# The second block's recurrence by pairs of tiles, its gates read from PSUM by ScalarE, its norm applied ahead, and output slabs begun three in step

## What is computed

```python
xn = rmsnorm(x, norm_mix_g)                    # the third norm of the whole kernel
u, g_lru, q, k, v, z = split(xn @ w_in)        # u, g_lru: 1024 wide each; z: 2048 (za, zb)
uc = conv4(u)                                  # centred depthwise convolution
r = sigmoid(uc @ wa + ba); i = sigmoid(uc @ wx + bx)       # 64-wide blocks, for each of two directions
a = exp(-8 * r * softplus(-lam)); beta = sqrt(1 - a * a)
h = scan(h_prev * a + beta * (i * uc))         # forwards and backwards over the tokens
y_a = (h_fwd + h_bwd) * gelu(g_lru)
y_b = banded_attention_with_sink(q, k, v)
merged = sigmoid(za + b) * y_a + sigmoid(zb + b) * y_b
x = x + merged @ w_out
x = x + (silu(gate) * up) @ w_ffn_out          # of rmsnorm(x) @ w_ffn_in
return rmsnorm(x, norm_final)
```

## Time and profile before

| | |
|---|---|
| median of 3 runs | 1547.47 us (1546.45 to 1548.66) |
| the profiled execution's own time | 1548.28 us |
| its span, first to last instruction | 1546.5 us |
| mean granted TensorE clock | 0.974 of full |
| busy: TensorE matmuls | 1448.2 us, 94% |
| busy: VectorE / ScalarE | 881.1 us, 57% / 638.3 us, 41% |
| DMA | 131.6 MB, mean 85 GB/s |

### The profile page before, as it was taken

One profiled execution on the slowest core, in us unless ns is written; L12 is line 12 of the kernel. 1 busy time (PEld: TensorE's weight loads), 2 busy tenths in 40 slices (PEclk: granted clock), 3 DMA queues, 4 the chain that ended last, 5 costly groups with the idle time before them and its releaser, 6 DMA issues.

```text
span 1546.5 us, 17781 instructions
## 1 busy us (share of the span) xinstructions
PE 1448.2 (94%) x7272; PEld 1166.9 (75%) x7272; DVE 881.1 (57%) x1267; ACT 638.3 (41%) x994; POOL 1.9 (0%) x7
## 2 busy tenths in 40 slices
PE   6997899998999999999899999978899999999997
PEld 6876577777778888888687777756678888888886
DVE  5775564566544445364647877578874443443445
ACT  4445465333222222123425667778743321222232
POOL 0000000000000000000000000000000000000000
PEclk9998899999999999999899999989999999999998
DMA  4211222222133323233131111122233332333323
GB/s 157 87 65 42 92 91 64 85 93 82 60 109 96 98 94 108 84 96 106 43 109 55 52 45 56 55 68 68 68 109 96 96 98 93 96 97 108 92 86 109
DMA packets 36561, 131.64 MB, mean 85 GB/s; under 512 B 4432, under 2 KB 4560, under 8 KB 36224
## 3 DMA queue, kind: packets, MB, share of 16 engines
q1 hardware_dynamic: 36128, 127.16, 26.4%
q0 software_dynamic: 352, 3.34, 0.6%
HBM read 128.39 MB, written 2.10 MB: 84 GB/s over the span
## 4 chain that ended last, share of the span: by engine, by line
PE 69%; DVE 16%; ACT 11%; issue 3%; DMA 1%; SPq 0%; DVEq 0%; ACTq 0%
PE gp L1351 20%; PE gp L1353 20%; PE gp L1352 20%; DVE w_lo L783 2%; PE mp L1527 1%; ACT arena L706 1%; PE mp L1538 1%; ACT w_hi L414 1%; DVE arena L1006 1%; PE mp L1499 1%; DVE arena L1013 1%; ACT a_hi L441 1%; ACT arena L563 1%; PE mp L1380 1%; ACT arena L710 1%
## 5 line engine op out<-in xcount | busy, mean ns | idle before, releaser
L1351 PE MATMUL gp<-a_hi,w_hi 128*128 128x512 f32 x1120 | 443.8, 396 | 14.2 <-DVE arena L1244 13.0
L1352 PE MATMUL gp<-a_lo,w_hi 128*128 128x512 f32 x1120 | 439.0, 392 | 0.0
L1353 PE MATMUL gp<-a_hi,w_lo 128*128 128x512 f32 x1120 | 438.3, 391 | 0.0
L783 DVE TENSOR_TENSOR w_lo<-raw,w_hi 128x1024 fp32r<-128x1024 f32 x232 | 283.5, 1223 | 168.1 <-ACT w_hi L414 166.9
L414 ACT ACTIVATE w_hi<-raw 128x1024 fp32r<-128x1024 f32 x232 | 243.3, 1052 | 197.3 <-PE gp L1353 105.1
L1351 PEld LDWEIGHTS gp<-a_hi,w_hi 128*128 128x128 f32 x1120 | 212.2, 189 | 66.5 <-DVE w_lo L783 16.5
L1353 PEld LDWEIGHTS gp<-a_hi,w_lo 128*128 128x128 f32 x1120 | 212.1, 189 | 45.1
L1352 PEld LDWEIGHTS gp<-a_lo,w_hi 128*128 128x128 f32 x1120 | 212.2, 189 | 42.6
L1351 PE MATMUL gp<-h_hi,w_hi 128*128 128x512 f32 x576 | 224.9, 390 | 8.9 <-DVE h_lo L817 3.5
L1353 PE MATMUL gp<-h_hi,w_lo 128*128 128x512 f32 x576 | 224.1, 389 | 0.0
L1352 PE MATMUL gp<-h_lo,w_hi 128*128 128x512 f32 x576 | 224.1, 389 | 0.0
(11 more groups left out here) (236 smaller groups left out, 1438.5 us busy)
## 6 DMA issues: line engine op xcount, KB each, us to landing
raw<-slabs SPq DMA_DIRECT2D x232, 512.0 KB, 3.5
arena<-x_in SPq DMA_DIRECT2D x4, 512.0 KB, 6.2
arena<-x_in POOLq DMA_DIRECT2D x1, 2048.0 KB, 8.2
out_t<-arena SPq DMA_DIRECT2D x8, 256.0 KB, 2.1
arena<-bias POOLq DMA_DIRECT2D x1, 1024.0 KB, 5.9
arena<-s5b SPq DMA_DIRECT2D x1, 512.0 KB, 9.1
arena<-s5c SPq DMA_DIRECT2D x1, 512.0 KB, 10.0
par<-params SPq DMA_DIRECT2D x1, 232.0 KB, 2.6
```

The source lines that it names most:

```text
L783: TT(w_lo[:, n % RING, :], raw[:, n % RAW, :], w_hi[:, n % RING, :].bitcast(F32), ALU.subtract).then_inc(w_lo_ready, 1)
L1351: pe.matmul(dst, hi, x_hi(t), start=t == 0, stop=False)
L1352: pe.matmul(dst, hi, x_lo(t), start=False, stop=False)
L1353: ins = pe.matmul(dst, lo, x_hi(t), start=False, stop=t == tiles - 1)
```

## The change

1. **Recurrence by pairs in two sets of buffers.** `lru[0]` and `lru[1]` each hold decay, input and beta for both directions. ScalarE takes the eight sigmoids of a pair, then its four tanh, four exponentials, two square roots; VectorE works on both directions in one 1024-wide instruction and scans into UC. HS is gone. The clamp at zero moves into the constant `decay_tanh`.
2. **Gates as they come.** ScalarE takes each gate product from PSUM as tanh of half of it (sigmoid(x) = (1 + tanh(x/2))/2), VectorE applies it with one instruction as (1 + tanh) * y, and the factor a half is in the split of the merged value. Likewise ScalarE takes u (copy) and g (gelu) from PSUM.
3. **The third norm applied ahead of 36 slabs** (16 of u and g, 20 of mix): VectorE multiplies x by gain and R and both engines split it into h, one chunk per slab beside the last eight q, k, v slabs. `uc` and the merged value are split into a, the fourth norm's input into h.
4. **Order of slabs.** `STAGE` replaces `MIX`: zb of tile 0 is multiplied inside attention's last unit, then each recurrence slab is followed by the four gate slabs of its own pair (three for the first).
5. **Outputs begin three in step** (`start_stage("out2", ..., 3, 5)`), with the third in an `mp` bank; splits run three ahead there.

The diff, cut to its core (the old bodies of the mix loops are in the listing above; the remaining hunks change counters and which of the buffers a and h is named):

```diff
@@ -61,6 +62,14 @@
 for _t in range(DC):
     MIX += ([("lru", _t // 2)] if _t % 2 == 0 else []) + [("zb", _t)] + ([("za", _t - 1)] if _t else [])
 MIX += [("za", DC - 1)]
+WINDOWS = [[("za", 0), ("zb", 1), ("za", 1)]]
+WINDOWS += [[(kind, t) for t in (2 * j, 2 * j + 1) for kind in ("zb", "za")] for j in range(1, DC // 2)]
+STAGE = [("zb", 0)]
+for _j, _gates in enumerate(WINDOWS):
+    STAGE += [("lru", _j)] + _gates
+assert sorted(STAGE) == sorted(MIX)
@@ -71,6 +80,8 @@
 ORDER = list(range(NSLAB))
 for _k in range(8):
     ORDER[SLAB["u2"] + 2 * _k], ORDER[SLAB["u2"] + 2 * _k + 1] = SLAB["u2"] + _k, SLAB["g2"] + _k
+for _i, _key in enumerate(STAGE):
+    ORDER[SLAB["mix"] + _i] = SLAB["mix"] + MIX.index(_key)
-MIX_SLAB = {key: SLAB["mix"] + i for i, key in enumerate(MIX)}
-MIX_OUT = {key: OUT["mix"] + i for i, key in enumerate(k for k in MIX if k[0] != "lru")}
-MIX_GATE = [g for t in range(1, DC + 1) for g in [("zb", t - 1)] + ([("za", t - 2)] if t > 1 else [])] + [("za", DC - 1)]
+MIX_SLAB = {key: SLAB["mix"] + i for i, key in enumerate(STAGE)}
+MIX_GATES = [key for key in STAGE if key[0] != "lru"]
+MIX_OUT = {key: OUT["mix"] + i for i, key in enumerate(MIX_GATES)}
...
-        HS = region(15360, DC, T)
         logit2 = [region(15360, 4, 3 * P), region(16896, 4, 3 * P)]
         PT2 = region(18432, 3, T)
         nd8 = region(19968, 3 * P)
-        lru = [region(12288 + T * i, T) for i in range(6)]
-        lru45 = region(12288 + 4 * T, 2 * T)
+        lru = [{key: region(12288 + 6 * T * i + 2 * T * x, 2, T) for x, key in enumerate(("decay", "input", "beta"))}
+               for i in range(2)]
...
+        START_OUT2 = 3
...
-                if _name in ("ff", "q2") and 2 <= _k < START_BANKS:
+                if _name in ("ff", "q2", "out2") and 2 <= _k < START_BANKS:
                     PLACE[_o] = mp, _k - 2
                 elif _name in ("gate_s", "u2", "g2"):
                     PLACE[_o] = gp, 0
+                elif _name == "mix":
+                    PLACE[_o] = gp, (_k + 1) % 2
                 else:
                     PLACE[_o] = gp, _o % 2
...
-            for n in range(SLAB["q2"] + START, SLAB["u2"]):
-                split(n + AHEAD)
+            for c in range(DC):
+                split(SLAB["q2"] + START + c + AHEAD)
+                act.wait_ge(h_norm, NORMALISED_AT + c + 1)
+                nc.scalar.activation(h_hi[:, c, :], tmp[c % 2], ACT.Copy).then_inc(h_hi_ready, 1)
...
             def inputs2(u):
                 m = u // 2
-                if u % 2:
-                    act.wait_ge(h_val, V_AT["uc"] + m + 1)
-                    nc.scalar.activation(h_hi[:, m, :], UC[:, m, :], ACT.Copy).then_inc(h_hi_ready, 1)
-                    act.wait_ge(out_read, OUT["u2"] + u + 1)
-                    nc.scalar.activation(G2[:, m, :], G2[:, m, :], ACT.Gelu_apprx_tanh).then_inc(gate_val, 1)
+                if u % 2 == 0:
+                    take("u2", u, tmp[m % 2])
+                    return
+                act.wait_ge(h_val, V_AT["uc"] + m + 1)
+                nc.scalar.activation(a_hi[:, m, :], UC[:, m, :], ACT.Copy).then_inc(a_hi_ready, 1)
+                take("u2", u, G2[:, m, :], func=ACT.Gelu_apprx_tanh)
             attention(att2, SLAB["u2"], inputs2)
...
+            ahead = itertools.count(SLAB["mix"] + AHEAD)
             def mix_gate(kind, t):
-                row, bias = {"za": (1, 0), "zb": (0, 8)}[kind]
-                act.wait_ge(out_read, MIX_OUT[kind, t] + 1)
-                nc.scalar.activation(tmp[row], tmp[row], ACT.Sigmoid, bias=col("b_gate", bias + t)).then_inc(gate_val, 1)
+                g, row = MIX_GATES.index((kind, t)), "ba".index(kind[1])
+                if t:
+                    act.wait_ge(gate_used, MIX_GATES.index((kind, t - 1)) + 1)
+                act.wait_ge(half_done, 2 * (MIX_SLAB[kind, t] + 1))
+                nc.scalar.activation(tmp[row], bank("mix", g), ACT.Tanh, bias=col("b_gate", 8 - 8 * row + t),
+                                     scale=0.5).then_inc(out_read, 1)
...
+                nc.scalar.activation(a_hi[:, t, :], Q2[:, t, :], ACT.Copy, scale=0.5).then_inc(a_hi_ready, 1)
+            def sigmoids(j, i):
+                t, tile = 2 * j + i, lru[i]
+                if t >= 2:
+                    act.wait_ge(lru_free, t - 1)
+                for q, (kind, name, d) in enumerate((("decay", "ba", 0), ("input", "bx", 0), ("decay", "ba", 1), ("input", "bx", 1))):
                     o = 4 * t + q
                     if o % 8 < 7:
                         act.wait_ge(lg_done, 7 * j + o % 8 + 1)
                     else:
                         act.wait_ge(half_done, 2 * (MIX_SLAB["lru", j] + 1))
-                    nc.scalar.activation(lru[row], mp[:, o % 6, :], ACT.Sigmoid,
+                    nc.scalar.activation(tile[kind][:, d, :], mp[:, o % 6, :], ACT.Sigmoid,
                                          bias=col(name, 8 * d + t)).then_inc(lru_sig, 1)
...
+            def decay_and_tanh(j):
+                act.wait_ge(lru_sig, 8 * j + 8)
+                for i in range(2):
+                    for d in range(2):
+                        ins = nc.scalar.activation(lru[i]["beta"][:, d, :], lru[i]["decay"][:, d, :], ACT.Tanh,
+                                                   scale=decay_tanh[:, 8 * d + 2 * j + i:8 * d + 2 * j + i + 1])
+                    ins.then_inc(lru_tanh, 1)
+                split(next(ahead))
+                for i in range(2):
+                    for d in range(2):
+                        ins = nc.scalar.activation(lru[i]["decay"][:, d, :], lru[i]["decay"][:, d, :], ACT.Exp,
+                                                   scale=decay_exp[:, 8 * d + 2 * j + i:8 * d + 2 * j + i + 1])
+                    ins.then_inc(lru_act, 1)
+            def roots(j):
+                for i in range(2):
+                    act.wait_ge(lru_tanh, 2 * j + i + 1)
+                    nc.scalar.activation(lru[i]["beta"], lru[i]["beta"], ACT.Sqrt).then_inc(lru_root, 1)
+            split(next(ahead))
+            mix_gate(*STAGE[0])
+            for j, gates in enumerate(WINDOWS):
+                sigmoids(j, 0)
+                split(next(ahead))
+                sigmoids(j, 1)
+                decay_and_tanh(j)
+                mix_gate(*gates[0])
+                roots(j)
+                split(next(ahead))
+                mix_gate(*gates[1])
+                if j:
+                    merged_hi(2 * j - 2)
+                    merged_hi(2 * j - 1)
+                for key in gates[2:]:
+                    split(next(ahead))
+                    mix_gate(*key)
+            split(next(ahead))
             merged_hi(DC - 2)
-            mix_gate("za", DC - 1)
             merged_hi(DC - 1)
             root_table()
             for k in range(DC):
-                split(SLAB["out2"] + AHEAD + k)
+                if k < DC - 1:
+                    split(SLAB["out2"] + START_OUT2 + k)
                 act.wait_ge(out_read, OUT["out2"] + k + 1)
                 xc = X[:, k, :]
-                nc.scalar.activation(a_hi[:, k, :], xc, ACT.Copy, scale=col("g_ffn2", k)).then_inc(a_hi_ready, 1)
+                nc.scalar.activation(h_hi[:, k, :], xc, ACT.Copy, scale=col("g_ffn2", k)).then_inc(h_hi_ready, 1)
                 square("n4", k, xc)
...
+            def normalised2(c):
+                if c >= 2:
+                    dve.wait_ge(h_lo_ready, H_AT["xn"] + c - 1)
+                STT(out=tmp[c % 2], in0=X[:, c, :], scalar=col("g_mix2", c), in1=R[:, :], op0=ALU.mult,
+                    op1=ALU.mult).then_inc(h_norm, 1)
+                if c:
+                    h_low(H_AT["xn"] + c - 1, c - 1, tmp[(c - 1) % 2])
             for m in range(START, DC):
                 evacuate("q2", m, Q2[:, m, :])
+                normalised2(m - START)
             for m in range(2):
                 evacuate("k2", m, KV2[:, m, :])
+                normalised2(4 + m)
             for m in range(2):
                 evacuate("v2", m, KV2[:, 2 + m, :])
+                normalised2(6 + m)
+            h_low(H_AT["xn"] + DC - 1, DC - 1, tmp[(DC - 1) % 2])
...
             V.up(TS(decay_exp, r[5], -8.0, None, ALU.mult))
-            TS(decay_tanh, r[5], 4.0, None, ALU.mult).then_inc(decay_ready, 1)
+            V.up(TS(col("b_gate", 0, 16), col("b_gate", 0, 16), 0.5, None, ALU.mult))
+            TS(decay_tanh, r[5], 4.0, 0.0, ALU.mult, ALU.max).then_inc(decay_ready, 1)
             def inputs2(u):
                 m = u // 2
+                split(SLAB["u2"] + AHEAD + u)
                 if u % 2:
-                    evacuate("u2", u, G2[:, m, :])
-                    h_low(H_AT["uc"] + m, m, UC[:, m, :])
+                    a_low("uc", m, UC[:, m, :])
                     return
                 x, y = tmp[m % 2], UC[:, m, :]
-                evacuate("u2", u, x)
                 dve.wait_ge(out_read, OUT["u2"] + u + 1)
...
+            ahead = itertools.count(SLAB["mix"] + AHEAD)
+            def apply_gate(kind, t):
```

(80 more changed lines are left out.)

121 lines of the change are left out of this document (26 added, 95 removed).

## The result

| | before | after |
|---|---|---|
| median of the runs of this comparison | 1548.12 us | 1551.35 us (1550.79 to 1553.40) |
| the profiled execution | 1548.28, span 1546.5 | 1552.31, span 1550.5 |
| mean granted TensorE clock | 0.974 | 0.974 |
| busy: TensorE / VectorE / ScalarE | 1448.2 / 881.1 / 638.3 us | 1450.9 / 863.7 / 631.2 us |

The changed kernel takes 1.0024 times as long (95% interval 1.0015 to 1.0034), 3.2 us more by the medians. I had forecast no change that can be told (1546.9, range 1539.5 to 1553.5). The time lies in the range, but 0.75 us above my own case (1544.4 to 1550.6), and the sign is wrong: a small gain was forecast, and a small loss was measured, with the whole interval above 1.

What follows compares the result with a forecast made beforehand. TensorE was taken to bound all but mix, where VectorE and ScalarE wait in turn. Full clock -6.7 us plus clock +6.1 gave -0.6 against the median of 1547.5: 1546.9 us, range 1539.5 to 1553.5.

Steps and rivals of the forecast that it cites:

- my own case: Whole kernel: time within 3.1 us of the forecast 1546.9, so 1544.4 to 1550.6; chance 0.39.
- u and gelu taken by ScalarE from PSUM: Attention: VectorE loses 16 operations, TensorE's three 0.4 us waits for ScalarE shrink; -1.2 us at best, bound 0, -1.2 taken.
- my sum of -0.6: Whole kernel: net change in us, from -6.7 at full clock and +6.1 for the slow clock.
- My sign of being wrong: Attention: longer than 161 us apart from its start would show the forecast wrong.
- The third norm ahead, +2.0: Attention's start: last tile's norm work delays the first logits, TensorE's wait grows from 1.47 to 3.5 us; +2.0 us.
- The round of a pair: Mix: VectorE 16.5, load 3.5 and ScalarE 14.0 us in one loop, 34.0 us per pair against 35.5.
- the opened loop: Mix, rival 2: loads land earlier, TensorE's 27.3 us sets the pair, saving up to 8 each, 1525 us; chance 0.04.
- The walk of the first pair: Mix: from the first recurrence slab, first sigmoids end at 6.0 us and the second recurrence slab's split at 26.5.
- The tail: Last pair and outputs: done 151.0 us after the first recurrence slab, loss 11.1 as before; starting three in step covers late low parts.
- No table load between exp and the gate's tanh: Mix, ScalarE: zero such loads taken, bound above 1.28 us per pair.
- The clock, +6.1: TensorE restarts after idling: of four, three or so cost the mean 1.9 us, plus 0.3 at the second recurrence slab.
- rival 3: Slow clock at all four restarts and the second recurrence slab, 12 to 13 us against -6.7: 1552 to 1554; chance 0.22.

Runs made afterwards that it cites:

- e1: The changed kernel, but VectorE copies u from PSUM itself, while gelu stays with ScalarE; 1550.53 us, 1.0018 of the kernel before.
- e11: The changed kernel with the edits of e3, e4 and e5 and a split ahead of the first tile's states, u still taken by ScalarE; 1532.12 us.
- e3: The changed kernel, but each third-norm product stands ahead of the copy beside it and the decay constants come earlier; 1546.63 us, 0.9995 of the kernel before.
- e4: The changed kernel, but VectorE splits the next recurrence slab ahead of the second tile's state work; 1543.63 us, 0.9975 of the kernel before.
- e5: The changed kernel, but outputs are made one after another, weights of outputs two and three split one step later; 1546.77 us, 1.0000 of the kernel before.

## Why the prediction was wrong, step by step

**The step that failed is "u and gelu taken by ScalarE from PSUM: -1.2 at best; bound 0".** Measured: +2.9 in the attention. I argued that the three waits of 0.4 us stood behind a gelu that waited for VectorE. They are there unchanged in e1 (1.1 us in three), where gelu comes straight from PSUM, so that was not their cause. And the work that VectorE lost was not free to move: u is the input of VectorE's own convolution, and ScalarE's queue delivers it behind exponentials that wait for VectorE. VectorE now waits for ScalarE where it had not (1.59 us at 852.12), and ScalarE then for VectorE (3.91 instead of 2.82). The bound of 0 excluded a loss by the words "where TensorE bounds"; VectorE's share of the stage is 78% (126.2 of 161.5 us), but its order was what mattered. e1 and e11 put 2.0 to 2.7 us on the copy of u; 0.7 is the wait for ScalarE's gelu in the first unit. With -1.2 replaced by +2.9, my sum of -0.6 becomes +3.5; the medians say +3.2. My sign of being wrong, an attention over 161 us, was set too high to catch it: my own terms gave 156.2, and it took 160.3.

**The third norm ahead, +2.0.** Right: the wait grew by 2.12 us. The slow restart behind it (1.55 left over in e3) was one of the four in the clock's +6.1. What I didn't see is that the order inside this step (the product behind the copy, the constants behind both), not the norm, cost it: e3 keeps the norm ahead and starts 1.3 us earlier than the kernel before.

**The round of a pair.** Right in what bounds it, partly by luck in its size. Second, third and fourth recurrence slab were put 26.5, 62.1 and 96.2 after the first and came at 25.2, 60.9 and 96.8. "The split stands behind both state blocks" was the argument against the opened loop, and e4 shows it as the cause: with the split ahead the pair falls to 30.8. The walk of the first pair was 1.3 too long: ScalarE's gate at 994.19 has no table load ahead of it and the sigmoids have one, so the first four sigmoids end 4.7 us after the slab's start and not 6.0. And a steady round was too short: 34.0 at full clock against 35.7 and 35.9. One term was left out of it, the table load ahead of the sigmoids. I had weighed it for the first pair only. ScalarE of the changed kernel:

```profile
1056.56 1.28 ACT L726 ACT_TABLE_LOAD   x1 [5.18 <-PE mp L1678]
1057.85 2.42 ACT L726 ACTIVATE arena<-mp,par 128x512 f32<-128x512 f32 x4
1060.14 1.08 ACT L425 ACTIVATE w_hi<-raw 128x1024 fp32r<-128x1024 f32 x1
```

The load begins only when the recurrence slab's first product is there, and the chain that ended last runs through it. ScalarE's split starts 5.31 us after the slab at 1054.83 and 5.02 after the one at 1090.74, where the walk has 3.5. In the kernel before the gates used the same function as these sigmoids, and no load stood there; now they use tanh. No run takes the load away, so its price of 1.3 in each of the two rounds that begin at the third and the fourth slab is read, not tested.

**The tail.** Three outputs were to be done at 151.0 plus its part of the clock, and were at 155.3 (1149.23 minus 993.95). The size is right only as a sum (see the clock below), the reading not: "starting three in step covers what the last tiles' late low parts cost" is refuted by e5: there these cost nothing, and without the start in step the tail is 4.9 us shorter. The pairs alone shorten the tail by 6.3 against before (90.55 to 84.21), and the new start gives 4.9 back. I compared the sum with the old one and took equality for a cover.

**No table load between exp and the gate's tanh.** Right: 4 loads in a pair of the changed kernel (L726, L740, L747, L708), and none between the exponentials and that gate.

**The clock, +6.1.** Near the total by luck, wrong in how. I let three or so restarts pay. By the rows six of eight stretches pay: from 1019.11 to the wait at 1044.86, 23.9 us for four slabs of 5.46, 2.1 lost; in the same way 0.3, 1.7, 1.9, 1.8 and 0.3 in the next five stretches, 3.9 at the outputs and 1.55 at the start, 13.5 us together (the 0.3 is lost also at a clock of 1.00, as behind 1044.86 and 1116.36). Against the walk at full clock only 4.3 (155.3 for 151.0) and the 1.55 reach the end, 5.9: a late gate slab shortens the wait behind it, as the argument against rival 3 had it. And the 4.3 are not the clock's alone: they hold two table loads that the walk left out (2.6) less the 1.3 by which its first pair was too long, so by this estimate the clock's part is nearer 3. That rival's condition was met in the gross sum, and its 1552 to 1554 is where the profiled execution lies, but not by its mechanism.

Where did the gain go? By the runs: the pairs gave 7.9 us (mix in e5 181.05 against 194.34 less the slab's 5.44), the start in step took 4.9 of it, the start of the attention 3.7, the copy of u and its company 2.9.
